# Two stacked transformer blocks in one kernel: reordered waits, other work at both ends, and one conditioning batch summed on VectorE

## The reference

```python
# first block, layer i = 0, 1
sh1, sc1, g1, sh2, sc2, g2 = split(silu(c) @ ada_w[i] + ada_b[i], 6)      # and the same from c_ctx
h = rmsnorm(x, norm_mix[i]) * (1 + sc1) + sh1
x = x + g1 * attention_i(h, hc)          # i = 0: differential attention, i = 1: neighbourhood attention
h2 = rmsnorm(x, norm_ffn[i]) * (1 + sc2) + sh2
x = x + g2 * conv_ffn(h2, ...)           # up (to 2 x 2816), 3-tap convolution, SiLU gate, down
# (layer 0 does the same for the context tokens)
x = rmsnorm(x, norm_out)
# second block, layer l = 0, 1
proj = rmsnorm(x, norm_g[l]) @ w_in[l]   # q, k, v, gates, merges, ... of four branches
x = x + (sum_i sigmoid(merge_i) * (branch_i @ w_branch[i])) @ w_out[l]
out = rmsnorm(x, final_norm_g)
```

## Time and profile before

| | before |
|---|---|
| median of 3 runs | 1644.51 us (1643.88 to 1645.31) |
| the profiled execution | 1647.73 us |
| its span in the trace | 1645.4 us |
| PE busy, share of the span | 1601.1 us, 97% |
| DVE, ACT, POOL busy | 922.3, 766.5, 542.8 us |
| mean granted clock of TensorE | 0.991 |
| transfers | 249.26 MB |

### The profile page before, as it was taken

One profiled execution on the slowest core, in us unless ns is written; L12 is line 12 of the kernel. 1 busy time (PEld: TensorE's weight loads), 2 busy tenths in 40 slices (PEclk: granted clock), 3 DMA queues, 4 the chain that ended last, 5 costly groups with the idle time before them and its releaser, 6 DMA issues.

```text
span 1645.4 us, 24642 instructions
## 1 busy us (share of the span) xinstructions
PE 1601.1 (97%) x9872; PEld 1348.4 (82%) x9872; DVE 922.3 (56%) x1477; ACT 766.5 (47%) x1408; POOL 542.8 (33%) x358
## 2 busy tenths in 40 slices
PE   7999998999999999999999999999999999999998
PEld 4777556777777888879767899999999999999987
DVE  3344475455423654342265888658476567768545
ACT  4323485354312443253375655445454555554553
POOL 2214144222211222221273111026224567423554
PEclk9999999999999999999999999999899999999999
DMA  9164510433155212364313654545434544533551
GB/s 396 65 245 163 214 43 27 174 133 146 69 198 214 94 70 75 127 210 155 120 35 132 257 179 167 172 173 181 144 129 154 179 154 174 199 129 129 179 197 59
DMA packets 52976, 249.26 MB, mean 151 GB/s; under 512 B 20608, under 2 KB 21760, under 8 KB 26368
## 3 DMA queue, kind: packets, MB, share of 16 engines
q1 hardware_dynamic: 44400, 244.42, 41.1%
q10 hardware_dynamic: 8464, 3.28, 0.8%
HBM read 246.63 MB, written 1.05 MB: 151 GB/s over the span
## 4 chain that ended last, share of the span: by engine, by line
PE 90%; DVE 6%; ACT 2%; issue 1%; DMA 1%; POOL 0%; POOLq 0%; DVEq 0%; ACTq 0%
PE psq L545 14%; PE psq L547 14%; PE psq L546 14%; PE psq L921 7%; PE ps L545 6%; PE ps L547 6%; PE ps L546 6%; PE psq L922 4%; PE ps L921 3%; PE ps L559 2%; PE ps L922 1%; DVE WL L527 1%; PE psq L1324 1%; PE ps L1352 1%; PE psq L2215 1%
## 5 line engine op out<-in xcount | busy, mean ns | idle before, releaser
L527 POOL TENSOR_TENSOR WL<-RAW,WH 128x1024 fp32r<-128x1024 f32 (+2 forms) x116 | 299.6, 2585 | 551.8 <-ACT WH L517 540.7
L527 DVE TENSOR_TENSOR WL<-RAW,WH 128x1024 fp32r<-128x1024 f32 (+3 forms) x264 | 323.8, 1251 | 272.5 <-ACT WH L517 272.3
L517 ACT ACTIVATE WH<-RAW 128x1024 fp32r<-128x1024 f32 (+2 forms) x380 | 361.0, 1001 | 166.8 <-DMA RAW<-wstream 116.4
L545 PE MATMUL psq<-NHL,WH 128*128 128x256 f32 (+1 forms) x1264 | 413.4, 327 | 5.3 <-DVE WL L527 2.5
L547 PE MATMUL psq<-NHL,WL 128*128 128x256 f32 (+1 forms) x1264 | 407.5, 322 | 0.0
L546 PE MATMUL psq<-NHL,WH 128*128 128x256 f32 (+1 forms) x1264 | 407.4, 322 | 0.0
L545 PEld LDWEIGHTS psq<-NHL,WH 128*128 128x128 f32 x1264 | 242.2, 192 | 34.6 <-issue 8.7
L547 PEld LDWEIGHTS psq<-NHL,WL 128*128 128x128 f32 x1264 | 242.1, 192 | 18.1
L546 PEld LDWEIGHTS psq<-NHL,WH 128*128 128x128 f32 x1264 | 242.1, 192 | 16.9
L921 PE MATMUL psq<-NHL,WH 128*128 128x512 f32 x416 | 148.6, 400 | 0.0
L545 PE MATMUL ps<-NHL,WH 128*128 128x256 f32 (+1 forms) x368 | 122.1, 332 | 0.0
(11 more groups left out here) (378 smaller groups left out, 2861.3 us busy)
## 6 DMA issues: line engine op xcount, KB each, us to landing
RAW<-wstream SPq DMA_DIRECT2D x196, 1024.0 KB, 4.9
RAW<-wstream SPq DMA_DIRECT2D x32, 704.0 KB, 4.0
K<-first SPq DMA_DIRECT2D x4, 1024.0 KB, 15.6
X<-xin SPq DMA_DIRECT2D x2, 1024.0 KB, 6.0
V<-first SPq DMA_DIRECT2D x2, 1024.0 KB, 19.0
Q<-first SPq DMA_DIRECT2D x2, 1024.0 KB, 25.0
BR<-rpb ACTq DMA_DIRECT2D x8, 256.0 KB, 7.7
BR<-rpb SPq DMA_DIRECT2D x8, 256.0 KB, 8.6
```

Of the source, the lines that this page charges most:

```text
L517: e.activation(WH[:, u % 3, a:z], RAW[:, v % 3, a:z], ACT.Copy).then_inc(w_hi, 1)
L527: e.tensor_tensor(WL[:, u % 3, a:z], RAW[:, v % 3, a:z], WH[:, u % 3, a:z].bitcast(F32), ALU.subtract).then_inc(w_lo_p if pool else w_lo_v, 1)
L545: e.matmul(o, lh, rh, start=start, stop=False)
```

## The change

- **Start:** DVE fills `FILL` with ones. PE multiplies it by itself (`pe_constant`: three times 512 columns and once 256, into a bank that is overwritten later), ahead of the first sums, and once more (256 columns) behind them.
- **First `qkv`:** for its last unit (u = 7) ACT does the rounding of the unit three ahead behind its output copies and the row copy of batch 1.
- **Attention of layer 0:** the tiles of ("wo", 0, 0) begin one step earlier and are six. Steps 38 to 42 take five tiles of ("wo", 0, 1). `pe_wo` does what is left of both.
- **Batch 4:** `dve_ada_step` multiplies each unit (128 x 2048) by its column of `silu(c)` and adds it to `WSUM`, and its end frees the ring's buffer. PE does one set of four products of ones with `WSUM` (`pe_ada_joint`) before the second `up` unit of the second half. The row copy, the transposes and the addition of the batch are moved to there.
- **Layer 1, `wo`:** `pe_ada(6, 0)` stands ahead of the sums of tiles 4 and 5.
- **Second block:** the scale row of norm 5 is copied to `RS_KEPT`. `dve_out_gain` reads it there and runs later, behind `dve_causal_max(0)`. `pe_compress_up` waits for the copy only. In both layers `lo_prep(vn)` stands between the additions of L1943.
- **End:** PE transposes X (two sets of eight transposes, beside the last two sums), DVE and ACT scale 512-column parts by the root, one value for each partition, and SP and ACT send them out with the tokens on the partitions. The spreading product is gone.

```diff
+JOINT_ADA = {("up", 0, HALF_FT + 1): (7,)}
     for m in range(DT):
-        run_ada(4, m)
         add(("down", 0, 0, m), 2)
         add_ada(4, m)
...
         def load_unit(e, v):
-            if v >= 3 and v - 3 not in SPLIT_AT:
+            if v >= 3 and KEYS[v - 3][:2] == ("ada", 4):
+                e.wait_ge(ada_acc, KEYS[v - 3][2] + 1)
+            elif v >= 3 and v - 3 not in SPLIT_AT:
...
+        def dve_ada_step(e, k):
+            v = UNIT_OF["ada", 4, k]
+            e.wait_ge(d_raw[v % 3], 16 * (v // 3 + 1))
+            if k == 0:
+                e.tensor_scalar(WSUM[:, :], RAW[:, v % 3, :], CB[:, k, 0:1], None, ALU.mult).then_inc(ada_acc, 1)
+                return
+            e.wait_ge(ada_acc, k)
+            e.scalar_tensor_tensor(out=WSUM[:, :], in0=RAW[:, v % 3, :], scalar=CB[:, k, 0:1], in1=WSUM[:, :],
+                                   op0=ALU.mult, op1=ALU.add).then_inc(ada_acc, 1)
+
+        def pe_ada_joint(e):
+            e.wait_ge(ada_par, 3)
+            e.wait_ge(ada_acc, 8)
+            for j in range(4):
+                mm = e.matmul(AB[32 * j:32 * j + 32, :], ONE.to_broadcast([P, 32]), WSUM[:, 512 * j:512 * j + 512],
+                              start=True, stop=True)
+            mm.then_inc(gemm, 1)
...
+        def pe_constant(e, o, n):
+            e.matmul(o[:, 0:n], FILL[:, 0:P], FILL[:, 0:n], start=True, stop=True)
+
         def pe_strip_sums(e):
-            e.wait_ge(c_zero, 3)
+            e.wait_ge(c_zero, 1)
+            for n in (512, 512, 512, 256):
+                pe_constant(e, bank[0], n)
+            e.wait_ge(c_zero, 4)
             for m in range(DT):
...
             mm.then_inc(strip_mm, 1)
+
+            pe_constant(e, bank[0], 256)
...
         def act_qkv(e, l):
-                split_hi(e, ahead(key))
+                if (l, u) != (0, 7):
+                    split_hi(e, ahead(key))
...
                 if l == 0 and i == 7:
                     act_ada_row(e, 1)
+                    split_hi(e, ahead(key))
...
         def pe_diff(e):
-                if 33 <= n < 38:
-                    if n == 33:
+                if 32 <= n < 38:
+                    if n == 32:
                         e.wait_ge(att_exp, 62)
-                    pe_abreast(e, ("wo", 0, 0), [bank[0], bank[1]], (n - 33,), pe_wait_heads)
+                    pe_abreast(e, ("wo", 0, 0), [bank[0], bank[1]], (n - 32,), pe_wait_heads)
+                if 38 <= n < 43:
+                    if n == 38:
+                        e.wait_ge(att_exp, 64)
+                    pe_abreast(e, ("wo", 0, 1), [bank[2], bank[3]], (n - 38,), pe_wait_heads)
...
         def pe_wo(e, l):
                     if i == 0:
-                        pe_abreast(e, ("wo", l, i), [bank[b], bank[b + 1]], range(5, DT), wait_x)
+                        pe_abreast(e, ("wo", l, i), [bank[b], bank[b + 1]], range(6, DT), wait_x)
+                    elif i == 1:
+                        pe_abreast(e, ("wo", l, i), [bank[b], bank[b + 1]], range(5, DT), lambda e, k: None)
...
+                if (l, i) == (1, 3):
+                    pe_ada(e, 6, 0)
                 for m in range(2 * i - 2, 2 * i):
                     if m >= 0:
                         pe_sums(e, n, m)
-            pe_ada(e, 6 if l else 3, 0)
+            if l == 0:
+                pe_ada(e, 3, 0)
...
         def pe_ffn(e, l):
                     if l == 0 and c == 1 and jj == 1:
+                        pe_ada_joint(e)
+                    if l == 0 and c == 1 and jj == 3:
                         pe_ada_turn(e, 4)
...
         def pe_down(e, l, c):
             for m in range(DT):
-                if l == 0 and c == 0:
-                    pe_ada(e, 4, m)
...
         def dve_ffn(e, l):
+                        if l == 0 and c == 0 and m == 0:
+                            dve_ada_step(e, 0)
                         if not (last and half):
                             split_lo(e, ahead(key), False)
+                        if l == 0 and c == 0 and m < DT - 1:
+                            dve_ada_step(e, m + 1)
...
+        def last_bank(q, half):
+            return ((bank[0], bank[4]), (bank[5], bank[7]))[q][half]
+
         def dve_last(e):
-            e.wait_ge(rs_bc, NORM_AT[7] + 1)
-            for a in range(4):
-                x = X[:, 2 * a:2 * a + 2, 0:256]
-                e.wait_ge(x_gain, 2 * a + 2)
-                e.tensor_tensor(x, x, NB[:, 0:256].unsqueeze(1).to_broadcast([P, 2, 256]), ALU.mult).then_inc(x_res, 1)
+            e.wait_ge(rs_done, NORM_AT[7] + 1)
+            for half in range(2):
+                e.wait_ge(last_tr, half + 1)
+                e.tensor_scalar(OUT_T[:, 0, 512 * half:512 * half + 512], last_bank(0, half), RS[:, 0:1], None,
+                                ALU.mult).then_inc(last_v, 1)
+
+        def act_last(e):
+            e.wait_ge(rs_done, NORM_AT[7] + 1)
+            for half in range(2):
+                e.wait_ge(last_tr, half + 1)
+                e.activation(OUT_T[:, 1, 512 * half:512 * half + 512], last_bank(1, half), ACT.Copy,
+                             scale=RS[:, 1:2]).then_inc(last_a, 1)
+                e.wait_ge(last_a, half + 1)
+                e.dma_start(out[:, 1, 512 * half:512 * half + 512],
+                            OUT_T[:, 1, 512 * half:512 * half + 512]).then_inc(d_out, 16)
...
         def dve_raw_norm(e, l):
+            if l == 0:
+                e.tensor_copy(RS_KEPT, NB[:, 256:512]).then_inc(rs_kept, 1)
...
         def dve_head(e, l):
+                if kind == 0:
+                    lo_prep(e, l, "vn", False)
             e.memset(FHL[:, 1024:1152].bitcast(U32), 0).then_inc(flat_lo, 1)
-            lo_prep(e, l, "vn", False)
...
-            if l == 0:
-                dve_out_gain(e, 5, "nout")
...
         def pe_compress_up(e, l):
-            e.wait_ge(x_res, X_BASE[6 + l])
+            e.wait_ge(rs_kept, 1)
...
                 pe_sums(e, n, 6)
+                pe_last_turns(e, 0)
                 pe_sums(e, n, 7)
+                pe_last_turns(e, 1)
+
+        def pe_last_turns(e, half):
+            if half == 0:
+                e.wait_ge(br_v, 32)
+                e.wait_ge(m_sum, 48)
+                e.wait_ge(x_res, x_ready(7, 5))
+            for m in range(4 * half, 4 * half + 4):
+                e.wait_ge(x_gain, m + 1)
+                for q in range(2):
+                    mm = e.transpose(last_bank(q, half)[:, (m % 4) * P:(m % 4) * P + P], X[:, m, q * P:q * P + P], IDENT)
+            mm.then_inc(last_tr, 1)
...
         def dve_layer(e, l):
             dve_causal_max(e, l, 0)
+            if l == 0:
+                dve_out_gain(e, 5, "nout")
...
         def dve_start(e):
+            e.memset(FILL, 1.0).then_inc(c_zero, 1)
...
-            pe_finish(e, 7)
```

More of the change, by code:

```diff
@@ L228, in unit_orders @@
             add(("out", l, i), 1)
-    for name, at, b in (("up", UP_ADA, 3), ("qkv", QKV_ADA, 5), ("up", LATE_ADA, 6)):
+    for name, at, b in (("up", UP_ADA, 3), ("qkv", QKV_ADA, 5), ("up", LATE_ADA, 6), ("up", JOINT_ADA, 4)):
         for key, ks in at.items():
@@ L399, in bass_two_block_decoder @@
             HL[0] = sb("HL0", [P, HALF_FT, 512], F32R, scope)
+            WSUM = sb("WSUM", [P, 2048], F32, scope)
         with ExitStack() as scope:
@@ L438, in const_at @@
             return CONST[:, CO[name] + a:CO[name] + a + n]
-        ONE32 = PP[:, 1, 0:32]
+        ONE32, FILL = PP[:, 1, 0:32], PP[:, 2, :]
         IDENT = const_at("ident", 0, 128)
@@ L465, in bass_two_block_decoder @@
         c_silu, c_zero, lam_v, lam_exp = (sem(n) for n in ("c_silu", "c_zero", "lam_v", "lam_exp"))
-        ada_row, ada_fin, ada_half, ada_par, amod = (sem(n) for n in ("ada_row", "ada_fin", "ada_half", "ada_par", "amod"))
+        ada_row, ada_fin, ada_half, ada_par, ada_acc, amod = (
+            sem(n) for n in ("ada_row", "ada_fin", "ada_half", "ada_par", "ada_acc", "amod"))
         x_res, x_low, x_sq, x_sq_v, sq_acc, sq_sum, g_pair = (
@@ L481, in bass_two_block_decoder @@
             sem(n) for n in ("sb_copy", "flat", "flat_hi", "flat_lo", "cm_zero"))
-        raw_hi, raw_lo, raw_copy, raw_rs, x_gain = (sem(n) for n in ("raw_hi", "raw_lo", "raw_copy", "raw_rs", "x_gain"))
+        raw_hi, raw_lo, raw_copy, raw_rs, rs_kept, x_gain = (
+            sem(n) for n in ("raw_hi", "raw_lo", "raw_copy", "raw_rs", "rs_kept", "x_gain"))
+        last_tr, last_v, last_a = (sem(n) for n in ("last_tr", "last_v", "last_a"))
         nrot_v, nrot_c, fx_v, fx_a, fx_tr, gs_a, gs_v = (
@@ L1642, in act_ffn @@
                         act_ada_row(e, 3)
+                    if l == 0 and c == 1 and jj == 1:
+                        act_ada_row(e, 4)
                     if l == 1 and jj == 4:
@@ L1652, in act_ffn @@
                         act_raw_hi(e, 0, m)
-                if l == 0 and c == 0:
-                    act_ada_row(e, 4)
         def dve_gate(e, l, U):
@@ L1681, in dve_ffn @@
```

(33 more changed lines are left out.)

## The result

The changed kernel takes 1631.4 us (median of 4 runs, 1630.4 to 1635.4), the kernel before 1644.3. The ratio is 0.9925, 95% interval 0.9908 to 0.9942: faster by 12.9 us, where 22.1 were forecast. That is inside the stated range of 1611 to 1634 us, but outside the forecast's own 1618 to 1627. The two profiled executions differ by 16.5 us (1647.73 and 1631.27), their spans by 16.3.

A forecast was written before the change was run, and what follows sets the result against it. PE, busy 97% of the span, was taken to bound the kernel, with its waits and the clock falls behind them. Eight terms summed to -22.1 us, from a median of 1644.5 to 1622.4 us; own range 1618 to 1627, stated range 1611 to 1634.

The forecast's parts named there:

- the clock still falls in layer 0: Rival, second block: the clock falls in layer 0 despite the change, 1630.8 us; chance 0.15.
- Batch 4: Down stretch: PE saves 6.9 us, but DVE's serial chain makes it wait 8.4 us in some five pieces; net +1.4.
- The ring keeps up: Rival, down stretch: low halves arrive in time and moving the sums to DVE gives its full -6.9, 1614.1 us; chance 0.20.
- The start: Start of the kernel: products of ones keep PE at dense work and raise the clock, -1.5 us (at most -3.6).
- First `qkv`, attention, layer 1's `wo`: Three places where PE's waits are filled or removed, the first two with clock falls: -4.1, -5.0 and -1.0 us.
- Time taken back later: Rival: time won early is half lost to weights that come no sooner, about 1628.5 us; chance 0.10.
- Layer 0 of the second block: First compression product no longer waits for dve_out_gain: -1.4 us of waits and -8.4 of clock, -9.8 in all.
- Layer 1: Second block, layer 1: gains from unit kf's low half alone, -0.9 us (0 to -1.3); cmp0's is the next late (0.64).
- if the clock falls in a new place: Condition, anywhere in the kernel, under which the forecast calls itself wrong; no size given.
- End: Kernel's end: two parts side by side on DVE and ACT replace four on DVE, -1.2 us (0 to -2).
- The offset: Whole kernel: the median of 1644.5 us lies 3.2 below the profiled execution, so 1625.6 becomes a median of 1622.4.

The follow-up runs named there:

- a_fill_the_wait: Changed kernel with 18 products of 128 columns, result overwritten, in PE's wait before layer 1's first compression product (second block): 1625.3 us.
- a_down_no_pool: Changed kernel with the second piece of the low half of the first half's eight down units on DVE, none on POOL: 1630.2 us.
- a_no_ones: Changed kernel without the products of ones at the start and the memset that feeds them: 1631.7 us.
- b_qkv_attention: Kernel before with only the change's edits to the first qkv's rounding and to layer 0's attention and wo tiles: 1635.9 us, ratio 0.9955.
- a_both_orders: Changed kernel with the batch 4 step ahead of the down unit's low half, and the first compression low half ahead of the turn of KN: 1613.0 us.
- `b_` edits: Edits of the kernel before that carry one part of the change: 1636.3 us (RS_KEPT and later dve_out_gain only), 1635.9 us (first qkv and attention only).
- a_batch4_on_pe: Changed kernel with batch 4 alone put back on PE, a set ahead of each down unit: 1632.6 us, ratio 0.9942 to the kernel before.

## Why the prediction was right, and where it was not

The direction and most terms held. The number is inside the wide range by luck in part: 1631.4 is next to the rival "the clock still falls in layer 0" (1630.8), but that isn't what happened. The clock fell in layer 1 instead, and the forecast's own range of 1618 to 1627 was missed. With the wait in layer 1 filled (`a_fill_the_wait`, 1625.3) the time lies inside it. Point by point:

- **Batch 4** ran by the forecast mechanism: the serial chain step, load, ACT, DVE, next step, with DVE standing still for POOL in every second unit (forecast periods 9.4 and 10.1 us, measured 9.3 and 9.9). The size was 1.4 us off, because the first step has one input and took 1.28 us instead of 2.3, the periods were a little shorter, and a set costs PE 1.18 and not 0.99 us. PE waited 5.9 us in three pieces, where 8.4 in some five were forecast. "The ring keeps up" was not what this code does, but the right order of two calls makes it true, and was worth more than its 6.9. The Trainium skill (SBUF — State Buffer, Who interferes with whom) has two SBUF inputs of DVE contend with GpSimd's reads, and whichever issues first hold the shared ports for its whole instruction. The trace agrees: 2.35 against 3.67 us, and `a_down_no_pool`.
- **The start**, -1.5: the -1.7 of the table can't be put down to the ones. `a_no_ones` says 0. The premise that the clock stays low without dense work came from one trace; four others without the ones have it up at the first set, near 13 us.
- **First `qkv`, attention, layer 1's `wo`**: as forecast in this pair of traces, and kept to the end. (The wait in attention is 2.5 us, so the clock fell after waits of up to 2.5, not of "2.4 us or less".) "Time taken back later" by loads is refuted by `b_qkv_attention` and `a_both_orders`. What can go again is clock: in layer 1's `wo` it fell in 5 of the 14 traces, two of the four of the kernel before and its `b_` edits and three of the ten of the changed one (0.90 or 0.95 in 880 to 915 us).
- **Layer 0 of the second block**: the mechanism held (wait gone, 37.0 us). The waits gave 2.6 us instead of 1.4, since the one on kf went whole. The clock gave 7.9 instead of 8.4, which is all that the forecast's own 44.9 and 37.0 leave. And both sizes are those of an execution in which the clock falls.
- **Layer 1** is the step that failed: "*Layer 1* gains from kf alone: -0.9 (0 to -1.3), because cmp0's low half is the next to be late (0.64)." It took the next wait (0.64) as fixed. But PE comes to it 1.3 us sooner and that low half came no sooner (0.3 us later), so two waits of 1.26 and 0.64 us became one of 2.39. The length alone is +0.3 us, where -0.9 was forecast; PE's idling in one piece let the clock fall, for 6.4. In all five traces with that wait unfilled the stage of layer 1 takes 43.3 to 44.9 us, in all nine others, with 1.26 and 0.6 us apart, with the wait filled or with none, 36.9 to 37.0. The text had the condition ("if the clock falls in a new place") and gave it no chance at this place.
- **End**: the tail behind the last sum became 1.1 us shorter, the transposes delayed that sum by 0.5.
- **The offset**: the forecast assumed that the profiled execution lies 3.2 us above the median for both kernels.

Left open: why the same wait lets the clock fall in one execution and not in the next (layer 0 of the second block in the kernel before, layer 1's `wo` in both kernels), and the longer load wait of `a_batch4_on_pe`.

## What to carry to other kernels

When a wait is taken away, work out when its engine now arrives at the next one: the new wait is about the sum of both, in one piece. Here one wait of 2.4 us cost 6 us more by the clock than waits of 1.26 and 0.64 us, 12 us apart. Where a release hangs on an in-order engine, put the releasing instruction ahead of any that waits for what it releases; here the swap of two calls was worth 8 us. Where a wait of PE can't be removed, products that nobody reads can hold the clock (6 us here for 18 of them, which filled 2.1 of 2.5 us).

## What the hardware showed that I had not expected

After the same waits the clock falls in one execution and not in the next: with waits of 1.26 and 1.5 us, 13 us apart, the stage took 44.9 us in two traces and 37.0 in a third. With one of 2.4 us it took 43.3 or more in five of five. In layer 1's `wo`, with the same wait of 1.81 us in the kernel before and its `b_` edits, it fell in two traces of four. In the down stretch the half speed sat after the second wait in five traces and after the last one before U11 in three, two of which have both, and at the start anywhere from 14 to 30 us. The Trainium skill (TensorE: Matmul & The Clock Gate, What's actually happening) says of the rise that it differs between runs of one kernel; here the fall does too, and the traces agree for the rise as well: the first set at the start took 1.93 us in one trace of the kernel before and 1.07 in the other. It would explain most of the kernel before's 1634 to 1652 us. A fall in a stretch where PE waits for a ring need not cost anything: the 3.4 us of half speed in the changed kernel's down stretch were covered, and as much behind the last wait cost 1.5 in `a_down_no_pool`.
